# A differential head's two maps are combined by DVE and POOL in two steps, and tail pieces move to later places

## The reference

```python
s = jnp.einsum('mbhqd,mbhkd->mbhqk', qblk, k) * scale + bias   # m: two maps
a = jax.nn.softmax(s, axis=-1)
w = a[0] - lam * a[1]                  # differential head: 8 of these
return jnp.einsum('bhqk,bhkd->bhqd', w, v)
...
o = rms_norm(o, norm_g) * (1.0 - lam_init)
...                                    # neighbourhood heads: 8, one map, a masked window of 256 keys
return jnp.concatenate([o_diff, o_na], axis=-1) @ w_out
...
x = layer_norm(alpha * x + h, ln1_g[l], ln1_b[l])
```

## Time and profile before

| what | us |
|---|---|
| median of 3 runs | 3393.82 (3392.39 to 3395.72) |
| the profiled execution, its own time | 3396.41 |
| its span, first to last instruction | 3394.6 |
| first attention stage, first maxima to last norm | about 176 to 383 |
| second attention stage, first maxima | 1859.0 |
| PE busy over the span | 3167.8 (93%) |
| DVE, ACT, POOL busy | 2480.7, 1233.7, 1090.5 |

### The profile page before, as it was taken

How to read it: one execution, slowest core, us unless ns; L and a number is a source line. 1 busy time by engine, 2 the same in 40 slices (tenths; PEclk the granted TensorE clock), 3 DMA queues, 4 the chain that set the end, 5 groups by cost and what they waited for, 6 DMA issues and landing times. The chain is left out here.

```text
span 3394.6 us, 48838 instructions
## 1 busy us (share of the span) xinstructions
PE 3167.8 (93%) x16726; PEld 2800.1 (82%) x16726; DVE 2480.7 (73%) x5112; ACT 1233.7 (36%) x1756; POOL 1090.5 (32%) x684
## 2 busy tenths in 40 slices
PE   7988799899899999999889888998999999999996
PEld 6866589898899999988677665898998999998885
DVE  3166389898688878778732654898978888787886
ACT  2365233344333333333223652333433333333332
POOL 0030056400355545433200301572004555454331
PEclk9989899999999999999999998999999999999998
DMA  7651225354999989889675422254569999898995
GB/s 260 139 131 60 89 83 175 134 235 187 364 347 349 347 319 340 308 316 352 218 268 126 113 81 76 97 174 166 193 235 365 360 340 336 317 343 287 338 353 180
DMA packets 334924, 806.17 MB, mean 237 GB/s; under 512 B 39312, under 2 KB 195472, under 8 KB 300208
## 3 DMA queue, kind: packets, MB, share of 16 engines
q1 hardware_dynamic: 258384, 525.31, 45.4%
q0 software_dynamic: 73728, 268.47, 21.2%
q10 hardware_dynamic: 2656, 10.49, 0.8%
HBM read 711.38 MB, written 99.09 MB: 239 GB/s over the span
## 5 line engine op out<-in xcount | busy, mean ns | idle before, releaser
L183 POOL DMA_INDIRECT g_ring<-in_peer_u,g_idx x256 | 365.4, 1427 | 793.8 <-DVE g_ring L193 744.4
L246 PE MATMUL o_bank<-v_hi,w_hi 128*128 128x512 f32 x1536 | 599.4, 390 | 16.5 <-DVE w_lo L1644 16.5
L247 PE MATMUL o_bank<-v_lo,w_hi 128*128 128x512 f32 x1536 | 600.4, 391 | 0.0
L248 PE MATMUL o_bank<-v_hi,w_lo 128*128 128x512 f32 x1536 | 600.2, 391 | 0.0
L183 POOL DMA_INDIRECT g_ring<-in_peer_v,g_idx x256 | 374.7, 1464 | 503.5 <-DVE x_sb L201 448.4
L1629 DVE TENSOR_TENSOR v_lo<-v_raw,v_hi 128x2048 fp32r<-128x2048 f32 x128 | 293.0, 2289 | 137.8 <-ACT v_hi L1564 137.4
L1564 ACT CAST v_hi<-v_raw 128x2048 fp32r<-128x2048 f32 x128 | 244.9, 1913 | 405.7 <-PE o_bank L248 386.4
L246 PE MATMUL h_bank<-x_hi,ws_hi 128*128 128x384 f32 x1152 | 385.7, 335 | 4.5 <-PEq L1312 4.5
L248 PE MATMUL h_bank<-x_hi,ws_lo 128*128 128x384 f32 x1152 | 385.7, 335 | 0.0
L247 PE MATMUL h_bank<-x_lo,ws_hi 128*128 128x384 f32 x1152 | 385.3, 334 | 0.0
L201 DVE SCALAR_TENSOR_TENSOR x_sb<-g_ring,g_h,x_sb 128x1024 f32<-128x1024 f32 x256 | 328.3, 1282 | 53.5 <-DMA g_ring<-in_peer_v,g_idx 36.3
(11 more groups left out here) (197 smaller groups left out, 6055.6 us busy)
## 6 DMA issues: line engine op xcount, KB each, us to landing
ws_raw<-in_uT SPq DMA_DIRECT2D x128, 1024.0 KB, 5.2
v_raw<-in_peer_v SPq DMA_DIRECT2D x128, 1024.0 KB, 6.9
gates_T<-gate_stage SPq DMA_DIRECT2D x12, 4096.0 KB, 12.6
g_raw<-gates_T SPq DMA_DIRECT2D x128, 384.0 KB, 8.9
w_raw<-in_w_in SPq DMA_DIRECT2D x24, 1024.0 KB, 9.2
ws_raw<-hidden_T SPq DMA_DIRECT2D x56, 384.0 KB, 4.7
w_out_half<-in_w_out SPq DMA_DIRECT2D x32, 512.0 KB, 3.5
ws_raw<-in_peer_wq SPq DMA_DIRECT2D x16, 1024.0 KB, 5.6
```

What stands on the lines that cost most here:

```text
L183: nc.gpsimd.indirect_dma_start(out=tail.ring[n % RING][:, :], out_offset=None, in_=table.rearrange("l e d -> (l e) d"), in_offset=bass.Ind ...
L246: nc.tensor.matmul(out, lh, rh, start=start, stop=False)
L247: nc.tensor.matmul(out, lh, rl, start=False, stop=False)
L248: return nc.tensor.matmul(out, ll, rh, start=False, stop=stop)
```

## The change

DVE no longer writes the sum of the two maps. It scales the second map in place and signals `factored`; POOL adds the second map to the first and signals `mixed`. The tail pieces of all engines stand at later units; the squares of both norms go to a free piece of the table `tb` in place of `catT`, and that of the layer norm is made in two halves whose sums DVE adds.

```diff
-        sq = catT[:, 0:DC // 2, :].rearrange("p c (h d) -> p (c h) d", d=HD)
+        squares = tb[:, NDH * T5_W:NDH * T5_W + NDH * HD]
+        sq = squares.rearrange("p (h d) -> p h d", d=HD)
         st = m.sb("ln_sums", [P, 2])
-        mv = m.sb("ln_mv", [P, 2])
+        mv = m.sb("ln_mv", [P, 3])
...
-        MULS = {f"mul_{n}": u for n, u in enumerate((24, 25, 26, 27, 29, 30, 31, 32))}
-        PE_SLOTS = {"turn_na": 20, "turn_diff": 23, **MULS}
-        ACT_SLOTS = {"square": 18, "turn_na": 21, "turn_diff": 24, "spread": 33}
-        DVE_SLOTS = {"read_diff": 18, "read_na": 19, "sums": 20, "gain": 22, "add_0": 28, "add_1": 33, "spread": 35,
-                     "norm": 37}
-        POOL_SLOTS = {"sums": 20, "spread": 35}
+        MULS = {f"mul_{n}": u for n, u in enumerate((26, 27, 28, 29, 31, 32, 33, 34))}
+        PE_SLOTS = {"turn_na": 21, "turn_diff": 24, **MULS}
+        ACT_SLOTS = {"square": 20, "turn_na": 23, "turn_diff": 26, "spread": 39}
+        DVE_SLOTS = {"read_diff": 19, "read_na": 20, "sums": 22, "gain": 24, "add_0": 32, "add_1": 37, "spread": 40,
+                     "norm": 42}
+        POOL_SLOTS = {"sums": 22, "spread": 40}
...
+            def add_maps(u):
+
+                pool.wait_ge(factored, NDH * (u // NH) + head(u) + 1)
+                nc.gpsimd.tensor_tensor(s[u % PB][:, 0, :], s[u % PB][:, 0, :], s[u % PB][:, 1, :],
+                                        ALU.add).then_inc(mixed, 1)
+
             def unit(u):
+                if 1 <= u <= UNITS and is_diff(u - 1):
+                    add_maps(u - 1)
...
-                        act.wait_ge(spread, qt)
+                        act.wait_ge(rms_asked, qt)
+                    if qt >= 2:
+                        act.wait_ge(spread, 2 * (qt - 1))
...
-                        act.wait_ge(rms_asked, qt + 1)
+                        if qt >= 1:
+                            act.wait_ge(hid, 2 * PIECES * qt)
...
-                    nc.scalar.activation(catT[:, :, :].rearrange("p a b -> p (a b)"), x[:, qt, :], ACT.Square,
-                                         bias=mv[:, 0:1], accum_out=mv[:, 1:2]).then_inc(spread, 1)
+                    act.wait_ge(rms_asked, min(qt + 2, TT))
+                    for i in range(2):
+                        if i == 1:
+                            act.wait_ge(spread, 2 * qt + 1)
+                        nc.scalar.activation(squares, x[:, qt, i * 512:(i + 1) * 512], ACT.Square, bias=mv[:, 0:1],
+                                             accum_out=mv[:, 1 + i:2 + i]).then_inc(spread, 1)
...
-                nc.vector.scalar_tensor_tensor(s[u % PB][:, 0, :], s[u % PB][:, 1, :], cf[:, 1:2],
-                                               s[u % PB][:, 0, :], ALU.mult, ALU.add).then_inc(mixed, 1)
+                nc.vector.tensor_scalar(s[u % PB][:, 1, :], s[u % PB][:, 1, :], cf[:, 1:2], None,
+                                        ALU.mult).then_inc(factored, 1)
...
-                    dve.wait_ge(spread, qt + 1)
+                    dve.wait_ge(spread, 2 * (qt + 1))
+                    chain.done(nc.vector.tensor_scalar(mv[:, 1:2], mv[:, 1:2], mv[:, 2:3], None, ALU.add))
+                    chain.wait()
```

More of the change, by code:

```diff
@@ L618, in attend @@
         turned, moved, summed = sem("a_turned"), sem("a_moved"), sem("a_summed")
+        factored = sem("a_factored")
         rms_asked, rms_done = sem("a_rms_asked"), sem("a_rms_done")
```

## The result

The changed kernel takes 3412.8 us (median of 4 runs, 3405.7 to 3416.7) beside 3393.4 for the kernel before: a ratio of 1.0053, interval 1.0038 to 1.0068. It is slower by 19 us, as forecast in sign; the forecast of 3423 was 10 us high, and the range held. The profiled execution is the longest of the four, 3416.7 us.

A forecast was written before the change was run, and what follows sets the result against it. PE was taken to bound the attention body, busy 109.0 of 125 us. Start +21, body -5 and end -1.5 made +14.5 us a layer, +29 for two layers: 3423 us, range 3402 to 3446.

The forecast's parts named there:

- The start: Stage start: head 0's addition waits behind POOL's 16 masks, transpose 21.4 us later; net +21 us a layer, bounds +17, +24.
- the term after it: Behind the first transpose: slow clock for 16 us, head 5 17 us behind head 0, 2 more; then 2 come back.
- The scaling and the addition: Differential head's path in steady state: scaling 0.40, addition 1.2, path 0.95 us longer; +4 us a layer, bounds 0 and 12.
- The sign of being wrong that I had named: Body: waits of PE for POOL's additions past 230 us that sum to over 6 us a layer.
- The later places: Tail pieces in the body: DVE's wait ahead of add_0 shrinks below 2 us; -9 us a layer.
- the small terms around it: Body: +2 for halved square and norm pieces, -2 of the other waits for maxima; whole body -5 us a layer.
- The end: End of the stage: last norm's reads come earlier, under two moved PE pieces; net -1.5 us, bounds -3 and +2.
- The sum: Whole kernel: +21 - 5 - 1.5 = +14.5 us a layer, +29 for two layers; 3423 us, 0.9% slower.
- POOL becomes the bound of a head: Rival: start as forecast, addition 1.7 us or scaling waits for POOL; +6 to +12 a layer, middle 3442; chance 0.22.
- The stretch that I feared for the scaling: DVE beside POOL: the one-tensor scaling contends for SBUF interfaces, or waits for POOL as L849 did (+1.0).
- The cheap-start rival: Clock doesn't fall or rises sooner at the start, body gives 8: +7 us a layer, 3408; chance 0.17.
- my forecast: Whole kernel: 3415 to 3432 us, around the forecast time 3423; chance 0.55.

The follow-up runs named there:

- e1: The kernel before, with one wait more: PE transposes each layer's first differential head only when all sixteen POOL masks are done; 3421.5 us, ratio 1.0088.
- e4: The changed kernel, but DVE alone mixes the first six heads of each layer and POOL adds only from the seventh unit on; 3388.0 us, ratio 0.9985.
- e5: The changed kernel with POOL's first-tile masks between the additions and later tiles' masks one by one behind the ninth to sixteenth unit; 3383.1 us, ratio 0.9969.
- e2: The changed kernel with DVE's old mixing and no addition on POOL; later places and halved square stay; 3370.6 us, ratio 0.9940.
- e3: The kernel before with scaling on DVE and addition on POOL, tail pieces at their old places; 3447.0 us, ratio 1.0169.
- e8: e4 with one more POOL addition of 256 columns into a spare tile ahead of each addition of the maps; 3405.6 us.
- e9: e2 with the eight masks of the later tiles moved on POOL to units 10 to 13; 3375.2 us.
- e7: e4 with POOL's addition cut to 256 columns in place of 512; 3373.3 us.

## Why the prediction came out

- *The start*: right in mechanism (e1, e4, e5), too large in size. The wait itself was 22.0 us for 21.4 forecast. What was mis-sized is the term after it: I had head 5 come 17 us behind head 0 at the slow clock, and a net +21 with bounds 17 and 24; it came 11.6 us behind it in the first layer and 13.8 in the second, and the net was +15.9, under the lower bound, and +17.8. The 16 us of slow clock that I carried over were counted from the stage's start: 5 of them lie ahead of the first transpose at 181.07, so behind it the slow level lasted 11 us before the change. Behind the changed kernel's first transpose it lasted 10.9 us in the second layer and 3.5 in the first (windows of the changed kernel, first layer; the column after POOL is the granted clock):

```profile
205.00:206.00 1.00, 0.98 (x3) 0.80 (x4) 0.93 (x5) 1.00 (x3) 0.00 (x0) 0.50 0.00 0
206.00:207.00 1.00, 0.95 (x5) 0.58 (x3) 0.72 (x2) 0.82 (x3) 0.49 (x1) 0.68 0.00 0
207.00:208.00 1.00, 0.54 (x4) 0.50 (x4) 1.00 (x5) 0.85 (x2) 0.78 (x1) 1.00 0.00 0
```

  That the first layer got away with 3.5 us is luck as far as the runs show (see the last section). The reading that the ninth head was transposed while POOL was still at its masks was off: 203.24 lies 0.9 us behind the end of the masks at 202.36. No term hangs on it.

- *The scaling and the addition*: 0.49 and 1.27 us against 0.40 and 1.2; the path grew by 1.1 us, not 0.95. The body's loss from it was put at 4 a layer. Beside e2 the body of the changed kernel is 4.7 us longer in the first layer and 1.0 shorter in the second, that of e4 5.3 longer and equal; the means of the two layers are 1.9 and 2.6, and the low clock of e2's second layer is in them. At the old places (e3) the loss is 9. The sign of being wrong that I had named, waits of PE for the additions past 230 us of over 6 us a layer, did come in the first layer:

```profile
PE Tb L957 <- POOL probs L732: 7.2, 9, 1.4
```

  At the same place of the second layer they sum to 5.8. The body was near the forecast all the same, because the waits behind the maxima fell from 13.8 to 4.6, as much as the 9 that the places were to give.
- *The later places*: -9 and the small terms around it, net -5 for the body, measured -5.4 and -6.2 once the 3.4 us of moved pieces are taken out. DVE's wait ahead of add_0 and add_1 went from 5.76 and 5.51 to 0.41 us in the first two of the three tiles; in the third it is 4.29 and 2.73, not under 2 as I had it.
- *The end*: -1.5 forecast, -2.3 and -2.6 measured, again without the 3.4.
- *The sum* was +29, measured +19 by the medians and +20 between the profiled executions; the start alone makes 8 of the 10 us. Body and end together gave 3.4 us more than forecast, and the 3 us outside the stages, for which I had no term, happen to cancel that.
- *The rivals*: that POOL becomes the bound of a head did not come about at its price of +6 to +12 a layer; the additions took 1.27 us in the median with six outliers of 1.65 to 2.24, each beside a DVE instruction on two SBUF tensors, and the scaling never more than 0.49. The stretch that I feared for the scaling went to the instruction ahead of it: at 211.89 the factor took 0.91 us in place of 0.22 and ended at 212.80, 0.01 after an addition that had begun at 211.52.

```profile
211.89 0.91 DVE L863 SCALAR_TENSOR_TENSOR map_factor<-map_factor,lam_work,rowsum 128x1 f32<-128x1 f32 x1
212.84 0.49 DVE L866 TENSOR_SCALAR probs<-probs,map_factor 128x512 f32<-128x512 f32 x1
```

```profile
211.52 1.27 POOL L732 TENSOR_TENSOR probs<-probs 128x512 f32<-128x512 f32 x1 [1.30 <-DVE probs L866]
```

  The mechanism that this rival needs does exist. In the changed kernel no scaling overlapped with a mask or an addition, so it had no chance to show. In e5 nine do, and eight of them take 0.92 to 1.45 us for 0.49; beside the ninth the mask began later than the scaling. In e8 it is 1.57 and more beside an addition. The rival lost because the two never met, not because they go together freely. The Trainium skill says in its page GPSIMD Engine Reference, in the table under Specifications, that GpSimd shares its SBUF interfaces with VectorE and that they contend where DVE runs in a two-port mode or reads two SBUF tensors. These scalings, which read one SBUF tensor, agree with the first half of that rule, as far as a duration can show it; the 1.71 us of e9's mixing, which reads two, agrees with the second.
- The cheap-start rival (3408) had its first half nearly right, a start of +17 (+15.9 and +17.8), but its mechanism, a clock that rises sooner than in the kernel before, came in the first layer alone. The measured 3412.8 lies 5 us above it and just under the 3415 to 3432 that I had called my forecast.

## What to carry to other kernels

Before work is handed to an engine that looks idle, read what stands ahead of it in that engine's program order: POOL was busy 9% of the body, and the wait behind its masks cost more (34 us up to the ninth transposes) than all the rest gained. Where a change has two parts, time each alone as well as together: here the later places alone are the best kernel (3370.6 us, 0.6% faster than before), and the split of the maps costs 42 us on top of them. A wait of one instruction for a slower engine is best given room by moving it: that is what the later places do. The length of a hand-over between engines counts too, though not in full: 0.54 us less on each of e7's 52 additions is 28 us of path, and 15 came back in time, part of it perhaps from DVE's shorter hold-ups.

## What the runs showed that I had not expected

After the same idle stretch of 22 us PE stayed at 1.2 GHz for 3.5 us in the first layer, while in the second layer of the same execution its transposes still took 1.06 us, the slow duration, at 1905.43, 9.8 us after the first at 1895.59, and the slow level lasted 10.9 us. In e1 and e3, which make PE stand still for 20 to 22 us in the same place, it lasted 9.3 to 11.2 us behind the first transpose in all four layers, and 11 in the kernel before, where PE doesn't stand still. So the 3.5 us are the exception. I can't say what sets the difference. It is as large as some effects measured here, and the runs of one kernel lie up to 20 us apart (e9: 3357.8 to 3377.9), so differences under 5 us between medians were not read.

The clock also differs in the body: 0.92 of full speed in e5's first layer and 0.97 in e4's, 0.94 and 0.97 in the two layers of e2, with PE busy 3 to 6 us longer at the lower values. Two parts of this comparison, the gain of the later places in the second layer and e5's body, carry that clock with them.
